# Setup stage of a streaming encoder step: load order, transposes and column products moved, every fourth low weight part on GpSimd

## The reference

```
m = jax.nn.silu(c) @ w + b            # w: 1024 x 3072, four of them
shift, scale, gate = jnp.split(m[:, None, :], 3, axis=-1)
h = rmsnorm(x, g) * (1 + scale) + shift
```

## Time and profile before

| | |
|---|---|
| median of 3 runs | 4101.99 us (4099.0 to 4108.2) |
| the profiled execution | 4112.55 us, its span 4111.0 us |
| TensorE matmul busy, whole program | 3575.6 us, 87% of the span |
| VectorE, ScalarE busy | 2129.3 us (52%), 1365.0 us (33%) |
| last instruction of the setup stage | ends 209.45 us from the start |

### The profile page before, as it was taken

The page is one execution under the profiler, slowest core; times in us unless marked ns, Lnnn a source line. Parts: engine busy times, 40 slices in busy tenths (PEclk is TensorE's granted clock), DMA queues, the critical chain, the costliest instruction groups (busy, mean ns, idle before and its releaser), DMA issues. The chain is left out here.

```text
span 4111.0 us, 53886 instructions
## 1 busy us (share of the span) xinstructions
PE 3575.6 (87%) x20685; PEld 2102.0 (51%) x20917; DVE 2129.3 (52%) x3527; ACT 1365.0 (33%) x2660; POOL 479.5 (12%) x1002
## 2 busy tenths in 40 slices
PE   6867888777697999999978888888888899999996
PEld 3535455544353555555534555555554455555553
DVE  4644444445445555555545554555544655555553
ACT  5534444344323122222124444444432222122122
POOL 0002122223110000000000222211200000000000
PEclk9888887778798999999989999999998999999998
DMA  7721122112311111111121333333331011111111
GB/s 290 276 59 59 58 83 75 54 47 62 102 35 45 38 47 41 37 47 42 40 66 38 115 115 110 115 105 111 106 114 55 29 47 42 37 47 41 37 37 47
DMA packets 222722, 303.33 MB, mean 74 GB/s; under 512 B 24848, under 2 KB 174969, under 8 KB 221910
## 3 DMA queue, kind: packets, MB, share of 16 engines
q1 hardware_dynamic: 193046, 190.24, 13.9%
q0 software_dynamic: 29504, 110.77, 8.4%
HBM read 264.23 MB, written 63.95 MB: 80 GB/s over the span
## 5 line engine op out<-in xcount | busy, mean ns | idle before, releaser
L96 PE MATMUL psum<-h,ffn_high 128*128 128x512 f32 (+1 forms) x2112 | 1035.9, 531 | 48.2 <-DVE hl L474 48.2
L98 PE MATMUL psum<-hl,ffn_high 128*128 128x512 bf16 (+1 forms) x2028 | 616.6, 337 | 0.0
L100 PE MATMUL psum<-h,ffn_low 128*128 128x512 bf16 (+1 forms) x2066 | 578.9, 332 | 2.9
L96 PE MATMUL psum<-actr,ffn_high 128*128 128x512 f32 (+1 forms) x1056 | 517.2, 530 | 15.7 <-DVE actl L807 15.7
L96 PEld LDWEIGHTS psum<-h,ffn_high 128*128 128x128 f32 x2112 | 409.4, 194 | 135.3 <-issue 43.9
L98 PEld LDWEIGHTS psum<-hl,ffn_high 128*128 128x128 bf16 x2112 | 206.3, 98 | 431.7 <-issue 372.8
L86 PE MATMUL psum<-h,attC_high 128*128 128x384 f32 x744 | 367.5, 494 | 40.2 <-DVE hl L474 23.2
L86 PE MATMUL psum<-h,attAB_high 128*128 128x384 f32 x648 | 333.6, 515 | 39.0 <-DVE hl L474 23.4
L784 DVE TENSOR_SCALAR y<-u,cvT 128x1168 f32<-128x1168 f32 x88 | 78.2, 888 | 530.0 <-ACT u L735 530.0
L98 PE MATMUL psum<-actl,ffn_high 128*128 128x512 bf16 (+1 forms) x1012 | 308.0, 337 | 0.0
L100 PE MATMUL psum<-actr,ffn_low 128*128 128x512 bf16 (+1 forms) x1034 | 290.3, 332 | 1.5
(11 more groups left out here) (441 smaller groups left out, 7129.6 us busy)
## 6 DMA issues: line engine op xcount, KB each, us to landing
ada_raw<-in_ada_w SPq DMA_DIRECT2D x48, 1024.0 KB, 7.7
ffn_raw<-in_w_up SPq DMA_DIRECT2D x88, 512.0 KB, 3.6
ffn_raw<-in_w_down SPq DMA_DIRECT2D x44, 512.0 KB, 3.7
raw_C<-in_cache_c_k POOLq DMA_DIRECT2D x64, 256.0 KB, 3.4
raw_C<-in_cache_c_v POOLq DMA_DIRECT2D x64, 256.0 KB, 3.0
out_ck_s<-in_cache_c_k POOLq DMA_DIRECT2D x8, 1984.0 KB, 8.7
out_cv_s<-in_cache_c_v POOLq DMA_DIRECT2D x8, 1984.0 KB, 14.3
attC_raw<-in_w_in_odd SPq DMA_DIRECT2D x24, 512.0 KB, 4.7
```

Of the source, the lines that this page charges most:

```text
L96: return pe.matmul(out, w, x[:, lo:hi], start=first and start, stop=last and stop, skip_group_check=True)
L98: return pe.matmul(out, top(w), xl[:, lo:hi], start=first and start, stop=last and stop, skip_group_check=True)
L100: return pe.matmul(out, wl, top(x[:, lo:hi]), start=first and start, stop=last and stop, skip_group_check=True)
```

## The change

- SyncE loads c and the constants, then chunks 0 to 5, then x, then chunks 6 to 47. The other small loads move to GpSimd's queue.
- The turns of x no longer stand in front: two follow the weight matmuls of each unit from the second to the tenth, and ScalarE's copies of them stand in the next unit. They use PSUM banks 4 and 5.
- The column products of a move behind the first unit of a + 1 (`columns(a - 1)`); the last ones stay at the end.
- The lambda products, the vector work and the modulation copies of VectorE move behind units or between chunks.
- GpSimd makes the low part of chunks 7, 11, ..., 47 (eleven of 48).

```diff
     @block.sync
...
         sp.dma_start(crow[0:1, :], ins["c_prompt"]).then_inc(S.c_in, 16)
         sp.dma_start(crow[1:NC9, :], ins["c_sample"]).then_inc(S.c_in, 16)
...
+        sp.dma_start(K[:, :], ins["consts"][:, 0:C_L]).then_inc(S.const_in, 16)
+        for c in range(6):
+            chunk(c)
         for t in range(0, QB, 2):
             sp.dma_start(xrow[:, t:t + 2, :], ins["x_prompt"][0, t * P:(t + 2) * P, :].rearrange("(t p) d -> p t d", p=P)
                          ).then_inc(S.x_in[t // 2], 16)
...
+        for c in range(6, FBASE):
+            chunk(c)
...
     @block.gpsimd
...
+        pool.dma_start(tab[:, :], ins["rel_bias"][0]).then_inc(S.tab_in, 16)
+        pool.dma_start(G.sinkp[:, :], ins["sinks"].broadcast_to([P, 8])).then_inc(S.sink_in, 16)
+        for c in range(7, FBASE, 4):
+            ring.split_low(pool, c)
+            if c % 12 != 7 or c == 7:
+                continue
+            a = c // 12
+            pool.wait_ge(S.mod_mm, a)
             pool.dma_start(msb[2 * NC9:2 * NC9 + 1, :], ada_b[a:a + 1, :]).then_inc(S.adab_in, 16)
...
     @block.scalar
...
+        for u, (a, j) in enumerate(units):
+            for k in range(KT // 2):
+                c = ada_chunk(a, j, k)
+                if c + 3 < FBASE:
+                    ring.split_high(act, c + 3)
+                if u and k % 2 == 0 and k // 2 < len(turns[u - 1]):
+                    x_evac(act, turns[u - 1][k // 2])
+            if u == 1:
+                act.wait_ge(S.lam_dot, 2)
+                act.activation(lams[:, 2:4], lams[:, 0:2], ACT.Exp).then_inc(S.lam_exp, 1)
+            last = ada_chunk(a, j, KT // 2 - 1)
+            act.wait_ge(S.f_used[last % 3], last // 3 + 1)
+            if a and j == 0:
+                act.wait_ge(S.mod_mm, a)
+            act.copy(msb[0:2 * NC9, j * D:(j + 1) * D],
...
     @block.tensor
...
+        for u, (a, j) in enumerate(units):
+            if u >= 2:
+                pe.wait_ge(S.ada_evac, u - 1)
+            for k in range(KT):
+                c = ada_chunk(a, j, k // 2)
+                w, wl = ring.ready(pe, c)
...
+            for q in turns[u]:
+                turn(q)
...
+            if a and j == 0:
+                columns(a - 1)
+        columns(3)
...
     @block.vector
...
+        for u, (a, j) in enumerate(units):
+            for k in range(KT // 2):
+                c = ada_chunk(a, j, k)
+                if c + 3 < FBASE and (c + 3 < 7 or (c + 3) % 4 != 3):
+                    ring.split_low(dve, c + 3)
+                if a and j == 1 and k == 1:
+                    modulation(a - 1)
```

More of the change, by code:

```diff
@@ L232, in setup, with x_bank, chunk @@
     ada_b = ins["ada_b"].rearrange("l s n -> (l s) n")
+    units = [(a, j) for a in range(4) for j in range(3)]
+    turns = [range(max(0, 2 * u - 2), min(18, 2 * u)) for u in range(len(units))]
+    def x_bank(q):
+        return ps[:, 4 + q % 2, :]
     @block.sync
     def _(sp):
-        sp.dma_start(K[:, :], ins["consts"][:, 0:C_L]).then_inc(S.const_in, 16)
-        sp.dma_start(maskf[:, :], ins["consts"][0:NB, C_L:C_N]).then_inc(S.const_in, 16)
+        def chunk(c):
+            a, j, k = c // (3 * KT // 2), c // (KT // 2) % 3, c % (KT // 2)
+            ring.load(sp, c, ada_w[a, j, k], view=("p (k n) -> p k n", dict(k=2)))
         sp.dma_start(crow[0:1, :], ins["c_prompt"]).then_inc(S.c_in, 16)
         sp.dma_start(crow[1:NC9, :], ins["c_sample"]).then_inc(S.c_in, 16)
[L240 to L252, removed]
+        sp.dma_start(K[:, :], ins["consts"][:, 0:C_L]).then_inc(S.const_in, 16)
+        for c in range(6):
+            chunk(c)
         for t in range(0, QB, 2):
@@ L297, in _ @@
             ring.split_high(act, c)
[L298 to L315, removed]
+        for u, (a, j) in enumerate(units):
[13 more added lines that the diff above has]
+            act.copy(msb[0:2 * NC9, j * D:(j + 1) * D],
+                     ps[0:2 * NC9, 2 * (u % 2):2 * (u % 2) + 2, :].rearrange("p b n -> p (b n)")).then_inc(S.ada_evac, 1)
     @block.tensor
     def _(pe):
-        pe.wait_ge(S.const_in, 32)
+        pe.wait_ge(S.const_in, 16)
         pe.wait_ge(S.csil, 1)
@@ L323, in _, with turn @@
         mm.then_inc(S.small_ready, 1)
[L324 to L330, removed]
+        pe.wait_ge(S.c_low, 2)
+        def turn(q):
             t, half = q // 2, q % 2
@@ L405, in _ @@
-        ch.then(dve.tensor_copy(cvT[:, :, :, :].rearrange("p l j t -> p (l j t)"), ps[:, 7, 64:416]))
-        dve.tensor_scalar(G.gsub[:, :], gT[:, 40:41], 1.0 - LAM_INIT, None, ALU.mult).then_inc(S.small_evac, 1)
-        for a in range(4):
-            for j in range(3):
-                for k in range(KT // 2):
-                    c = ada_chunk(a, j, k)
-                    if c + 3 < FBASE:
-                        ring.split_low(dve, c + 3)
+        for c in range(3):
+            ring.split_low(dve, c)
@@ new lines, in lambdas @@
+        def lambdas():
+            dve.wait_ge(S.lam_in, 64)
+            for j in range(2):
+                dve.tensor_tensor_reduce(out=lamp[:, j, :], in0=lamv[:, 2 * j, :], in1=lamv[:, 2 * j + 1, :], scale=1.0,
+                                         scalar=0.0, op0=ALU.mult, op1=ALU.add,
+                                         accum_out=lams[:, j:j + 1]).then_inc(S.lam_dot, 1)
+            dve.wait_ge(S.tab_in, 16)
+            dve.tensor_scalar(rev[:, P:384], tab[:, 255::-1], tab[:, 256:257], 1.0 / SCALE, ALU.subtract,
+                              ALU.mult).then_inc(S.rev_made, 1)
```

120 lines of the change are left out of this document (62 added, 58 removed).

## The result

| | before | changed |
|---|---|---|
| median of 13 runs each | 4102.65 us (4090.28 to 4108.2) | 4114.48 us (4109.0 to 4123.37) |
| ratio | | 1.0033, 95% interval 1.0023 to 1.0043 |
| profiled execution | 4112.55 us | 4109.7 us, span 4107.8 us |
| end of the setup stage | 209.45 us | 220.48 us |

The change makes the kernel slower by 0.33%, some 12 us (forecast: 4113). The stage ends 11.0 us later (forecast: 220.4 us, 11 later). The two profiled executions alone would say otherwise: that of the changed kernel is 3 us shorter. Runs of one kernel are 14 to 18 us apart, so for the total the medians count, and for the stage its own end. The stage end is read in one profiled execution of each kernel; how much it differs between executions of one kernel no run shows.

The account below looks back on a forecast made before the run. VectorE's subtraction was the pace; GpSimd's chunk would lengthen the unit. Chunk 7 at 42.5, cycles 122, clock 12, columns 31, end 12.9 make 220.4 us, 11 later: 4102 + 11 = 4113 us, range 4076 to 4137.

Parts of the forecast that it names:

- The bound before, and the start: Setup stage: VectorE's subtraction paces units at 9.2 us; with weights loaded first, TensorE begins chunk 7 at 42.5 us.
- GpSimd's low part: GpSimd's subtraction of 2,048 numbers: taken as 4.7 us, bounds 2.4 and 6.2 us.
- The middle bound: GpSimd's subtraction if its two inputs are read one after the other: 4.3 us.
- The cycle: Steps in a row from one unit's first-chunk use to the next, through GpSimd's fourth chunk: 12.2 us against 9.2.
- The clock's share: TensorE's waits halve its clock during the fourth chunk and turns: 0 to 2.4 us per cycle, 1.2 taken.
- Every other path is shorter: Per unit, DMA 10.0 us, ScalarE 9.8 and VectorE 6.9 all stay below the 12.2 us cycle.
- The column products: Three blocks on TensorE behind a first unit lie on the path in full: 10.4 us each, lower bound 7.66.
- A: Rival: GpSimd's low part is quicker, 2.9 or 2.4 us, giving 4081 or 4076 us; chance 0.18.
- B: Rival: GpSimd takes 4.7 us but TensorE's clock holds, 23 us less, 4090 us; chance 0.10.
- C: Rival: no change, GpSimd's low part at about 3.9 us, 4102 us give or take 7; chance 0.18.
- D: Rival: GpSimd and VectorE lock each other out, cycle grows by 2.3 us ten times, 4136 us; chance 0.12.
- The bias transfers cost nothing.: SyncE's bias transfers behind the last load, costed at nothing; next in line if the stage shrank over 6 us.

Follow-up runs that it names:

- the order alone: Changed kernel with VectorE making all 48 low parts again, none on GpSimd: stage end 184.60 us, median 4082.16 us, -0.55% against the kernel before.
- the run at half the width: Changed kernel with GpSimd subtracting only the first 1,024 of 2,048 columns of its chunks: stage end 179.39 us, median 4080.35 us.
- the run with the turns in the wait: Changed kernel with the two turns of x ahead of the fourth chunk on TensorE, not behind the unit: stage end 206.38 us, median 4103.77 us.

## Why the prediction was right

*The bound before, and the start.* Weights first is a gain, as read from the earlier trace rows: with the order alone chunk 7's low part is there 18 us earlier. But in the changed kernel it came at 46.65, not 42.5. The step that failed is "at 421 GB/s a chunk takes 2.5 us: chunk 5 at 19.5". ScalarE began chunk 5 at 23.78, and most of the loss stands between chunk 2 (13.31) and chunk 3 (18.62), 5.3 us apart instead of 2.5. That is where the small loads on GpSimd's queue, costed at nothing, run beside the large ones: 1.6 of 4.2 us are shown to be the lambda loads, the rest is open.

*GpSimd's low part.* 4.7 was taken, 4.56 measured (11 operations, 4.51 to 4.73). The Trainium skill, GPSIMD Engine Reference, section 3.1, gives 4,497 ns; this case's trace agrees within 1.3%. The middle bound, 4.3 for two reads one after the other, came nearest, and 2.1 ns per column is a little over twice the fill's 0.93; that it is two reads in a row fits, but no run tries it.

*The cycle.* The row of steps is right, item by item, and GpSimd's operation lies in it with its full length, as the run at half the width shows. At full clock the row is 11.55 us (the run with filler matmuls), not 12.2: two turns take 0.8 there, not 1.18, since a pair overlaps its neighbours, and GpSimd 0.14 less. The clock's share is the reverse: 1.6 per cycle instead of 1.2, for the fourth chunk and the turns took 4.23 us where 2.65 is full clock. Two errors of opposite sign leave 13.15 against 13.4. TensorE's idle time before the fourth chunk, worked out at 3.5, was 2.7 to 3.6 us behind the start. "Every other path is shorter" holds for the kernel as changed, but the other paths were misjudged. The one over ScalarE (cast, msb copy, cast) is as long as the row at full clock, which the run with the turns in the wait shows; the prediction counted ScalarE's work only as a sum. And the DMA's 10.0 and ScalarE's 9.8 are no lower limits of a unit: with the order alone and with the half width units of 9.4 us were measured.

*The column products.* "10.4 each" was mis-sized: the three blocks took 8.28, 8.48 and 7.30 us, since their first part ran at full clock. But a cycle with a block is 21.9 to 23.5 us long, 8.7 to 10.3 above one without, as half clock follows the block. Together 28 us, against 31.

*The ledger*, in us:

| | predicted | measured |
|---|---|---|
| chunk 7 starts on TensorE | 42.5 | 46.7 |
| ten cycles without the blocks | 134 | 132.7 |
| three blocks with what follows them | 31 | 27.9 |
| from chunk 47 on TensorE to the end | 12.9 | 13.2 |
| end of the stage | 220.4 | 220.5 |

The end is hit to 0.1 us because errors of +4.2, -1.3, -3.1 and +0.3 cancel: that is luck. The sign does not hang on that; the last digits do.

*The rivals.* A, at half the width, is what its sum said: 183 for 2.4 us, the run 179.39, the 10.0 us of the DMA being 9.4. B was tried by force: with the clock mostly up the stage ends at 202.1, 18 us earlier, where 23 had been worked out. C was the price of 3.9 us, which GpSimd did not have. D, the lock, is there in both directions, and costs this kernel nothing that the rows show, as the order of the lists had said. VectorE's rows while GpSimd makes the low parts of chunks 15 and 23:

```profile
70.01 4.49 DVE L418 SCALAR_TENSOR_TENSOR columns<-consts,columns 128x1 f32<-128x1 f32 x1
...
75.88 2.28 DVE L182 TENSOR_TENSOR ada_low<-ada_raw,ada_high 128x2048 bf16<-128x2048 f32 x1
```
```profile
108.64 4.45 DVE L182 TENSOR_TENSOR ada_low<-ada_raw,ada_high 128x2048 bf16<-128x2048 f32 x1 [3.14 <-ACT ada_high L177]
```

L418 is one number per partition, and lasts 0.20 us alone (in the kernel before and with the order alone); here it ends at 74.50, when GpSimd's 69.77 + 4.73 ends. The 2.29 us of L182 become 4.45: asked for at 108.64, GpSimd done at 110.96, ended at 113.09. So what no row before showed, that VectorE waits behind GpSimd, these rows do. The Trainium skill, SBUF — State Buffer, section "SBUF: two separate sides", says that whichever starts first keeps the port pair for its whole instruction, and this case agrees in both directions: GpSimd's 5.61 us behind VectorE's pair is the other one. It does not lengthen the stage here, since VectorE has only three low parts per cycle of 13 us: apart from the start, TensorE waits for VectorE once more, 0.67 us, in the whole stage.

*"The bias transfers cost nothing."* Right: done 25.1 us ahead.

## What to carry to other kernels

Work given to a slower engine costs where it closes a loop: here a ring three deep ties the fourth chunk's low part to the next unit's first, so 2.3 us more on it, with the half clock that the longer wait brought, became some 3.5 us per unit (13.15 against 9.4 to 10.0 with the order alone), although VectorE was relieved of nearly a quarter of its low parts. Try the parts of a change apart: this one held a gain of 0.55% under a larger loss. When an experiment hits its number, check the mechanism too: moving the turns gave the stage end that was expected, but by the clock. And look at what stays behind the small matmuls on TensorE: cut into two blocks they cost less than in one, cut into six with weight matmuls between them more.

## What the hardware showed that was not expected

- With small matmuls strewn among large ones the granted clock fell to 0.50 and stayed there to the end of the unit in two of three units (step 3.86 us for 2.11), and stood at 1.00 in the other, with the same instructions. Why one unit escapes is not settled.
- Ten matmuls of filler in a wait of some 3 us raised the mean granted clock from 0.80 to 0.91, and the stage ended 18 us earlier.
- A VectorE operation on one number per partition (0.20 us alone) lasted 4.49 us beside GpSimd's subtraction, and 2.32 us beside that of half the width, ending with it both times: such rows are waits, though the profile counts them as busy time (VectorE's mean for L182 rises from 2.29 to 2.81 us).
- With a DMA share of 1.14 the engines moved 247 GB/s while small broadcast packets ran among the large ones, 352 in the same stretch with one row per lambda load, and 420 from 20 us on.
